# Attention of a hybrid decoder: query blocks of 112 rows with two key chunks, scores from stacked fp16 halves, three steps of lead, and V turned inside the q projection

## The reference, cut to what matters

```python
q = (hn @ w_q).reshape(bsz, seq_len, N_KV_HEADS, Q_PER_KV, ATTN_HEAD_DIM) * scale
s_meta = jnp.einsum("bnqkgd,bmkd->bnkgqm", qb, km)
s_band = jnp.where(mask, jnp.einsum("bnqkgd,bnskd->bnkgqs", qb, kband), NEG_INF)
s_sink = jnp.broadcast_to(sink[None, :, :, None, None], s_meta.shape[:-1] + (1,))
p = softmax(concatenate([s_meta, s_band, s_sink], -1))
ob = einsum("bnkgqm,bmkd->bnqkgd", p[..., :N_META], vm) + einsum("bnkgqs,bnskd->bnqkgd", p[..., N_META:N_META + 2 * BLOCK], vband)
```

## Time and profile before

| | |
|---|---|
| median of 3 runs | 2880.36 us (2878.78 to 2881.43) |
| the profiled execution | 2882.5 us, its span 2880.5 us |
| PE busy | 2706.8 us, 94% |
| DVE busy | 1440.2 us, 50% |
| ACT busy | 942.2 us, 33% |
| POOL busy | 736.5 us, 26% |
| mean granted clock of PE | 0.974 |

### The profile page before, as it was taken

How to read it: one execution, slowest core, us unless ns; L and a number is a source line. 1 busy time by engine, 2 the same in 40 slices (tenths; PEclk the granted TensorE clock), 3 DMA queues, 4 the chain that set the end, 5 groups by cost and what they waited for, 6 DMA issues and landing times.

```text
span 2880.5 us, 44637 instructions
## 1 busy us (share of the span) xinstructions
PE 2706.8 (94%) x17764; PEld 1776.4 (62%) x17764; DVE 1440.2 (50%) x1763; ACT 942.2 (33%) x1729; POOL 736.5 (26%) x476
## 2 busy tenths in 40 slices
PE   7899999999997999999999789898969999999996
PEld 5566666666664666666666456454636666666664
DVE  6576767686767544455111741554175444553113
ACT  4333333343414333222111452565242233232111
POOL 1043435353253101001212410232450010011214
PEclk9999999999998999999999999899989999999998
DMA  2101101011120111111111011000101111111111
GB/s 103 44 30 37 37 30 38 30 37 35 57 87 22 51 46 48 51 51 59 51 50 45 15 37 51 1 1 1 44 15 51 49 46 51 51 54 52 49 50 59
DMA packets 37979, 123.74 MB, mean 43 GB/s; under 512 B 3312, under 2 KB 12656, under 8 KB 37872
## 3 DMA queue, kind: packets, MB, share of 16 engines
q1 hardware_dynamic: 37872, 122.25, 13.1%
HBM read 118.04 MB, written 4.19 MB: 42 GB/s over the span
## 4 chain that ended last, share of the span: by engine, by line
PE 81%; DVE 8%; ACT 5%; DVEq 2%; issue 1%; POOL 1%; POOLq 0%; ACTq 0%; DMA 0%
PE PS L1504 24%; PE PS L1505 24%; PE PS L1506 24%; PE PS L1676 2%; DVEq L1459 2%; ACT TT L989 1%; DVE UB L1075 1%; PE PS L1593 1%; DVE small L1460 1%; DVE R L1064 1%; POOL hT L524 1%; PE PS L1683 1%; PE PS L1706 1%; PE PS L1668 1%; ACT BIG L989 1%
## 5 line engine op out<-in xcount | busy, mean ns | idle before, releaser
L1504 PE MATMUL PS<-R,whi 128*128 128x384 f16 (+1 forms) x3360 | 1048.5, 312 | 29.3 <-DVE wlo L1052 18.1
L1505 PE MATMUL PS<-R,whi 128*128 128x384 f16 (+1 forms) x3360 | 1048.2, 312 | 0.0
L1506 PE MATMUL PS<-R,wlo 128*128 128x384 f16 (+1 forms) x3360 | 1048.0, 312 | 0.0
L1052 DVE SCALAR_TENSOR_TENSOR wlo<-stage,whi 128x1024 f16<-128x1024 f32 (+1 forms) x196 | 264.3, 1349 | 981.0 <-ACT whi L569 981.0
L1504 PE MATMUL PS<-BIG,whi 128*128 128x384 f16 (+1 forms) x1632 | 508.6, 312 | 10.6 <-DVE wlo L1052 8.1
L1505 PE MATMUL PS<-BIG,whi 128*128 128x384 f16 (+1 forms) x1632 | 508.5, 312 | 0.0
L1506 PE MATMUL PS<-BIG,wlo 128*128 128x384 f16 (+1 forms) x1632 | 508.4, 312 | 0.0
L1504 PEld LDWEIGHTS PS<-R,whi 128*128 128x128 f16 x3360 | 330.6, 98 | 205.9 <-issue 23.4
L1505 PEld LDWEIGHTS PS<-R,whi 128*128 128x128 f16 x3360 | 330.4, 98 | 172.6 <-issue 10.4
L1506 PEld LDWEIGHTS PS<-R,wlo 128*128 128x128 f16 x3360 | 330.5, 98 | 167.4 <-issue 2.0
L530 POOL TENSOR_TENSOR BIG<-TT,BIG 128x1040 f32 x44 | 95.0, 2159 | 854.7 <-ACT BIG L938 854.7
(11 more groups left out here) (223 smaller groups left out, 2813.7 us busy)
## 6 DMA issues: line engine op xcount, KB each, us to landing
stage<-wa SPq DMA_DIRECT2D x164, 512.0 KB, 3.5
stage<-wd SPq DMA_DIRECT2D x32, 704.0 KB, 4.0
hT<-h SPq DMA_DIRECT2D x4, 1536.0 KB, 11.4
out<-hT SPq DMA_DIRECT2D x2, 1536.0 KB, 5.8
hT<-h SPq DMA_DIRECT2D x2, 1088.0 KB, 6.4
out<-hT SPq DMA_DIRECT2D x1, 1024.0 KB, 4.7
pr<-prm SPq DMA_DIRECT2D x1, 328.0 KB, 6.4
BIG<-wdt SPq DMA_DIRECT2D x1, 128.0 KB, 10.3
```

The lines of the kernel that those rows point to most:

```text
L1052: eng.scalar_tensor_tensor(out=wlo[:, slot, 0:width], in0=stage[:, slot, 0:width], scalar=WS, in1=whi[:, slot, 0:width], op0=ALU.mult, op1 ...
L1504: eng.matmul(acc, whi[:, slot, ws], x(0, k, b), start=first, stop=False)
L1505: eng.matmul(acc, whi[:, slot, ws], x(1, k, b), start=False, stop=False)
L1506: return eng.matmul(acc, wlo[:, slot, ws], x(0, k, b), start=False, stop=last)
```

## The change

Everything happens from the K/V stage to the end of the attention. Nothing else in the program moves.

- **Blocks.** 112 queries instead of 128 in blocks 0 to 8, and a last block of 32 queries: the 16 meta tokens and the last 16. There are 40 steps: 4 with 128 keys, 32 with 256 keys, 4 with 160 keys. The first of two key chunks is the 16 meta keys and the 112 before the block's own window, the second the 128 from there on.
- **Scores.** Q lies in `q_stack` as fp16, its rounded half on one half of the partitions and the remainder on the other. K lies in `k_part(0)` rounded and `k_part(1)` remainder, each on both halves. A head's scores are two fp16 products of 128 rows per piece of keys, and from block 2 on there are two pieces, of 16 and 240 keys. Scores have two sets of banks (0, 1 and 2, 3).
- **Writing K and Q.** ACT writes the rounded half, and DVE the remainder from PSUM. For K both write both halves of the partitions. The semaphores `kq_hi` and `kq_lo` tie them. ACT waits at each block for DVE's remainder of the block before, and only then counts it in `evac`.
- **V.** 18 windows instead of 9 chunks (10 of the blocks' own windows, 8 of 128 rows whose first 16 POOL then overwrites with the meta rows). One is turned behind each of the first 18 column blocks of the q projection, and ACT copies it in the same place. The q projection is written out, no loop.
- **Lead.** PE's scores run three steps ahead, DVE's masks two. The probabilities have four buffers, `values` has banks 6 and 7 by turns, and the probabilities are all in `BIG`.
- **Fewer pieces.** Eight transposes instead of twelve, one copy of 896 columns without a drain instead of two copies with one, and four products of values instead of six. The output of blocks 2 and 5 crosses a column block and is written in two pieces, that of the last block too.

```diff
+QB = P - META
+NQB = (SEQ + QB - 1) // QB
+LEAD = 3
+        def q_stack(h, a, z):
+            return QS[:, h * L + a:h * L + z]
+        def k_part(part, g, a, z):
+            o = (2 * g + part) * L
+            return KS[:, o + a:o + z]
-        SM = [TT[:, :, :].rearrange("p a b -> p (a b)")[:, 1088 * i:1088 * i + 1088] for i in range(2)]
+        SM = [BIG[:, i, 0:1024] for i in range(4)]
+        def key_pieces(b):
+            if b == 0:
+                return [(0, 0, P)]
+            if b == 1:
+                return [(0, 0, P), (P, QB, QB + P)]
+            return [(0, 0, META), (META, QB * (b - 1), QB * (b - 1) + keys(b) - META)]
+        V_WIN = [(QB * b, own_keys(b)) for b in range(NQB)] + [(QB * c - META, P) for c in range(1, NQB - 1)]
...
                     if i < 2:
+                        if 3 * i + b > 0:
+                            eng.wait_ge(kq_lo, 3 * i + b)
+                            eng.sem_inc(evac, 1)
                         for hh in range(2):
                             for to in range(2):
+                                r = eng.activation(k_part(0, 2 * i + hh, s, s + n)[64 * to:64 * to + 64],
+                                                   PS[64 * hh:64 * hh + 64, bank, 0:n], ACT.Copy, scale=1.0 / WS)
+                        r.then_inc(kq_hi, 1)
...
+                if i < 2:
+                    for b, (s, n) in enumerate(BLK):
+                        eng.wait_ge(kq_hi, 3 * i + b + 1)
+                        for hh in range(2):
+                            own = slice(64 * hh, 64 * hh + 64)
+                            for to in range(2):
+                                r = eng.scalar_tensor_tensor(out=k_part(1, 2 * i + hh, s, s + n)[64 * to:64 * to + 64],
+                                                             in0=PS[own, 3 * i + b, 0:n], scalar=1.0 / WS,
+                                                             in1=k_part(0, 2 * i + hh, s, s + n)[own],
+                                                             op0=ALU.mult, op1=ALU.subtract)
+                        r.then_inc(kq_lo, 1)
                 split_lo(U_KV + i + 3, i % 2)
...
-                if n >= 3:
-                    eng.wait_ge(probs_turned, n - 2)
-                eng.tensor_tensor(probs(n), PS[0:T, 0:4, 0:w], mask[0:T, :].unsqueeze(1).broadcast_to([T, QPK, w]),
+                if n >= 4:
+                    eng.wait_ge(probs_turned, n - 3)
+                eng.tensor_tensor(probs(n), score_acc(n, 0, w), mask[0:T, :].unsqueeze(1).broadcast_to([T, QPK, w]),
...
             masked(0)
+            masked(1)
             for n in range(NQD):
-                if n + 1 < NQD:
-                    masked(n + 1)
+                if n + 2 < NQD:
+                    masked(n + 2)
                 denominators(n)
                 if n > 1:
                     out_lo(n - 2)
...
+            for i in range(KD):
+                for b in range(3):
+                    tile(U_Q + i, 3 * (J_Q + i), i % 2, i % 2, x_big, x_norm=3, blocks=(b,))
+                    if 3 * i + b < len(V_WIN):
+                        v_turn(3 * i + b)
...
-                if n > 0:
-                    eng.wait_ge(scores_masked, n)
+                if n > 1:
+                    eng.wait_ge(scores_masked, n - 1)
...
+                    for o, a, z in key_pieces(b):
+                        for part_ in range(2):
+                            m_ = eng.matmul(score_acc(n, o, o + z - a)[:, r, :], q_, k_part(part_, g, a, z),
+                                            start=(part_ == 0), stop=(part_ == 1))
...
-                if n > 0:
-                    eng.wait_ge(out_lo_ready, n)
+                if n > 1:
+                    eng.wait_ge(out_lo_ready, n - 1)
...
-            scores(0)
-            scores(1)
+            for n in range(LEAD):
+                scores(n)
             for n in range(NQD):
-                if n + 2 < NQD:
-                    scores(n + 2)
+                if n + LEAD < NQD:
+                    scores(n + LEAD)
                 transposes(n)
                 if n > 0:
                     values(n - 1)
```

More of the change, by code:

```diff
@@ L321, in probs @@
         def probs(n):
             b = QCH[n][0]
-            T = CHUNK[b][1]
-            return SM[n % 3][0:T, 0:QPK * keys(b)].rearrange("p (r w) -> p r w", r=QPK)
-        def soft(n, i):
[L327 to L333, removed]
+            T, w = queries(b), keys(b)
+            return SM[n % 4][0:T, 0:QPK * w].rearrange("p (r w) -> p r w", r=QPK)
@@ new lines, in score_acc, with out_pieces @@
+        def score_acc(n, w0, w1):
+            T = queries(QCH[n][0])
+            o = 1024 * (n % 2)
+            return PSf[0:T, o:o + 1024].rearrange("p (r w) -> p r w", r=QPK)[:, :, w0:w1]
+        def soft(n, i):
+            return small[0:queries(QCH[n][0]), n % 4, i, :]
+        def out_pieces(n):
+            b = QCH[n][0]
+            if b == NQB - 1:
+                return [(0, 0, 0, META), (META, 2, L - META, META)]
+            t0, pieces = META + QB * b, []
+            for i, (s, w) in enumerate(BLK):
+                a, z = max(t0, s), min(t0 + QB, s + w)
+                if a < z:
+                    pieces.append((a - t0, i, a, z - a))
+            return pieces
@@ L973, in _ @@
                 eng.wait_ge(v_turned, c + 1)
-                eng.activation(VR[0:T, c, :], PS[0:T, 6 + c % 2, 0:256], ACT.Copy).then_inc(v_copied, 1)
-            with eng.Fori(0, KD // 2) as i:
-                for e in range(2):
-                    for b, (s, n) in enumerate(BLK):
-                        evacuate(i * 6 + 3 * (J_Q + e), e, b, BIG[:, ds(i * 2 + (KD + e), 1), s:s + n],
-                                 1.0 / (WS * AD ** 0.5))
-                    split_hi(i * 16 + units_loaded(U_Q + e + 2, e), e)
+                eng.activation(v_rows(c)[0:T, :], PS[0:T, 6 + c % 2, 0:256], ACT.Copy).then_inc(v_copied, 1)
@@ L1821, in _, with v_turn @@
             eng.wait_ge(evac, 6 + 3 * (J_KV + 4))
-            for c, (t0, T) in enumerate(CHUNK):
+            def v_turn(c):
+                t0, T = V_WIN[c]
                 if c >= 2:
@@ L1827, in _ @@
                 r.then_inc(v_turned, 1)
-            with eng.Fori(0, KD // 2) as i:
-                for e in range(2):
-                    tile(i * 2 + (U_Q + e), i * 6 + 3 * (J_Q + e), e, e, x_big, x_norm=3)
+            for i in range(KD):
+                for b in range(3):
+                    tile(U_Q + i, 3 * (J_Q + i), i % 2, i % 2, x_big, x_norm=3, blocks=(b,))
+                    if 3 * i + b < len(V_WIN):
+                        v_turn(3 * i + b)
             eng.wait_ge(evac, 6 + 3 * (J_Q + KD))
```

203 lines of the change are left out of this document (126 added, 77 removed).

## The result

The changed kernel takes 2884.86 us (median of 20 runs) against 2880.34 us of the kernel before (20 runs). The ratio is 1.0015, with a 95% interval of 1.0008 to 1.0022, so it is slower by 4.5 us. One of its runs, at 3575 us and a mean granted clock of 0.74, stands outside the ratio, as does one of 3344 us among those with V turned ahead. The forecast was 2878.5, which is 1.9 faster. The value lies in the range and under the likeliest case (within 0.2%), but the sign of the sum was wrong.

The account below looks back on a forecast made before the run. No engine was full; DVE and ACT working in turn set the attention's 6.28 us step. Terms 1.0 + 4.0 + 0.6 - 7.5 = -1.9 us took 2882.5 to 2880.6, less 2.1 for the median: 2878.5 us, range 2864 to 2900.

Parts of the forecast that it names:

- the likeliest case: Whole kernel: no measurable change, within about 0.2%, 2874.6 to 2886.1 us; chance 0.38.
- K/V stage, the step that failed: K/V stage: ACT and DVE alternate on K, delaying weights; net +1.0 us, -2 with cheap prices, +6 with dear ones.
- 4 x 0.31 + 4 x 0.36 + 2 x (4 x 0.40 + 4 x 0.47): K/V stage: ACT's copies and DVE's remainders of one K unit; 9.9 us with about 0.3 of handing over.
- V in the q projection: q projection: 18 windows of two transposes are paid in full on PE; +4.0 us, 7 at the other end.
- Both terms of this stretch together: q projection to first mask: V's transposes +4.0 us and the later first mask +0.6 us; 4.6 forecast.
- Lead and chain: Attention, full steps: a chain through two steps, 10.5 to 10.7 us per two, 5.3 a step; scores off it.
- the rival in which the lead doesn't loosen the chain: Attention: steps stay at about 6.0 us, +22, 2901 us; chance 0.17 shared with dear preparation.
- the rival of the dissolved chain: Attention: odd and even steps slide, busiest engine sets 4.4 us a step; 29 us more gain, 2850; chance 0.12.
- The sum of the attention: First mask to last output: 212.2 us against 219.7, so -7.5, with full steps 32 x 5.3 = 169.6.
- The rival of the falling clock: Attention: at 1.2 GHz a step needs 8.3 us instead of 5.3; a third of them costs 32, 2911; chance 0.12.
- Contention of DVE and POOL: Attention: DVE's mask and maximum run beside POOL's product without slowing, nothing added; otherwise 16 us more.
- The signs that I had named: Third K/V weights 2 to 4 us later, PEclk 1.0; refuted by pairs outside 9.5-11.5, maxima over 1.25, q projection over 91 us.

Follow-up runs that it names:

- V turned ahead: Changed kernel with all 18 windows of V turned in a row ahead of the q projection; 2887.38 us, ratio 1.0028.
- The half copies: Changed kernel writing only the own 64 rows of each K head, high and low, so scores are not the reference's; 2870.76 us, ratio 0.9967.
- the filling: Changed kernel with six more unused products of 240 columns on PE ahead of each step's transposes; 2878.75 us, ratio 0.9993.
- the denominators first: Changed kernel, three steps of lead, with denominators(n) ahead of masked(n + 2) in DVE's loop; 2827.25 us, ratio 0.9823.
- ACT straight through the K units: Changed kernel with ACT copying all three K blocks without waiting for DVE's remainders, one wait behind the weight half; 2871.47 us, ratio 0.9974.

## Why the prediction was wrong, point by point

- **K/V stage, the step that failed.** The forecast had +1.0 and the stage gave +5.6, near the dear end of +6. The mechanism was right: ACT and DVE alternate, the third unit's weights are late, the fourth's twice as late, and V's turning no longer stands ahead of q. What was mis-sized is the term "4 x 0.31 + 4 x 0.36 + 2 x (4 x 0.40 + 4 x 0.47)". A copy by ACT took 0.395 and 0.49 us, a remainder by DVE 0.45 and 0.565 (1.58, 1.97, 1.79 and 2.26 us for four). That is 12.2 instead of 9.9 us per unit; it counts twice, and the difference of 4.6 us is the whole error of the stage. With it the forecast's -1.9 would have been +2.7, so this term alone turned the sign. For ACT I had the 0.49 in hand, from the very row that did the same job before, and argued it down by the new destination's layout. For DVE I took off 0.08 for overlap, and its copies came out above even my dear bounds of 0.42 and 0.55. In the groups of four neither discount appeared. The half copies confirm the size: leaving out 6.0 us per unit brought the fourth unit's start 11.9 us forward and shortened the stage by 12.7.
- **V in the q projection: right.** Forecast +4.0, measured 3.9 against the version without it. Both terms of this stretch together, 4.6, stand against 4.7.
- **Lead and chain: right for the regular pairs.** Forecast 10.5 to 10.7 us per two steps, measured 10.49 in a regular pair and 10.8 on average. The scores, put off the chain, came onto it at half clock. POOL took 1.90, as priced. Two steps of lead gave 6.03, the "about 6.0" of the rival in which the lead doesn't loosen the chain. The reason given against the rival of the dissolved chain, that the order on DVE ties the denominators to a later mask, is shown by the swap of these two.
- **The sum of the attention: right by two errors.** From the fifth mask (1815.76) to the 37th (1988.53) it took 172.8 us, which is the forecast's 169.6 + 2 + 1.2. But the clock, forecast at 1.0, was 0.79. With the filling, at 0.95, the same stretch took 167.0, so the forecast was some 6 us too long for a full clock, and the lowered clock happened to make that up. That is luck. The rival of the falling clock had the fall right and its price wrong. It let a step at half clock take 8.3 us, about twice the 4.3 that I had given PE. From the run with the denominators first PE needs about 3.2 us a step at full clock, twice which is 6.4 (an estimate), and the clock never stayed at the half level for long: the lowest window of 10 us shown here has 0.59. In a regular pair the new scores take 2.3 us at half clock and only just reach the other branch.
- **Contention of DVE and POOL: right.** The mask at 1906.92 and the maximum at 1908.22 lie beside POOL's product of 1906.01 to 1907.91 and take 1.21 and 1.22 us, as they do with POOL idle. By the Trainium skill, "SBUF — State Buffer", "Who interferes with whom", DVE instructions that read at most one SBUF operand, outside the modes that take both ports, don't contend with GpSimd; this trace agrees.
- **The sum.** With the measured stages the terms give 5.6 + 4.7 - 8.2 = +2.1 where the forecast had -1.9. The medians say +4.5. The 2.4 us between the two are not assigned to a place: one profile each stands for 20 executions, and the stage's start alone differs by up to 6.7 us between executions.
- **The signs that I had named.** The third unit's weights were ready 4.9 us later in the stage (forecast 2.7, the sign 2 to 4), since one K part was 2.3 us longer than priced. The clock was 0.79 and not 1.0, and three pairs of steps lay outside 9.5 to 11.5 us, with 9.16, 12.17 and 11.53. These three spoke against me. The maxima took 1.22 us, and the q projection 88.8 us from its first product to its last copy, both inside their bounds.

The size of what was left on the table was not seen at all. The forecast named the tie on DVE and took it as given; a swap of two lines was worth thirty times the forecast's own effect.

## What to carry to other kernels

Where two engines hand blocks to each other in turn, price the instructions at the pitch of the row that does the same job already, without discount, and count every one twice if the unit repeats; then ask whether the handing over is needed at all. When software pipelining deepens a lead, each engine's loop has to be ordered anew: work whose inputs are long there goes ahead of work for a later step, and the same order is wrong with a shorter lead. A second branch that is "hidden" by a microsecond is one clock level away from being the chain, so both branches of a fork are to be written down with their lengths at either level.

## What the runs showed of the hardware that was not expected

- The same loop ran at either level of PE's clock. In the changed kernel the granted clock of windows of 10 us was 0.59 to 0.94, with PE busy for 6.6 to 9.3 us of them. In the regular pairs the transposes behind a wait of 2.56 us begin at full clock (starts 0.10 apart from 1908.28), and the values behind them run at the half one (four take 1.00 us, 0.60 in the following step). The scores behind those take 2.29 us, and those of the following step 1.44 again. With ACT straight through the K units the same loop, with waits of 2.60 and 1.35 us in each pair, stayed at 1.00 from 1840 to 1880 and fell to 0.83 and lower after that. So these runs don't show what made it fall. With the denominators first, in steps of 3.77 us with a pause of 0.5 us, it stayed at 1.00. The Trainium skill, "TensorE: Matmul & The Clock Gate", "A second HAM failure mode: psum-queue depth-cycling", tells of a kernel whose clock swings between its two levels through frequent short idle times of PE. The trace here agrees in kind, in that the clock swings between two levels in a loop with short idle times, and the price was about 5 us in 175.
- Copies of 64 partitions out of PSUM have no gap and no overlap worth counting: ACT 0.395 us for 272 and 0.49 for 384 columns, DVE 0.45 and 0.565 (in groups of four).
- GpSimd copied 64 x 1040 fp16 values across the halves of the partitions in 1.05 us (two of the eight took 1.83 and 1.92), and the kernel's time lost nothing by it. The two slow ones each overlapped a DVE weight remainder, which reads two SBUF tiles (`stage` and `whi`), and one of these remainders took 1.99 us instead of 1.23.
